# Slot tables of a two-layer hybrid trunk kernel: attention tiles, modulation blocks, first merge level and v products at other slots, solved blocks written back one weight unit earlier in layer 1, decay rows loaded at a later slot

## What is computed

```python
mod_lat = jax.nn.silu(c) @ w_ada + b_ada                 # also for c_ctx
p = (rmsnorm(x, norm_w) * (1.0 + sc) + sh) @ w_in        # combined projection
a = p[:, :, 0] - lam * p[:, :, 1]                        # group A: two softmaxes, then @ v
m = einsum(k_beta, k) * decay; m = tril(m, -1) + eye     # group B: gated delta rule, chunks
sol = triangular_solve(m, rhs)                           # then a scan over the chunks, both ways
x = x + gt * (concat([y_a, y_b]) @ w_out)
```

## Time and profile before

| | |
|---|---|
| median of 3 runs | 2437.49 us (2430.56 to 2441.39) |
| the profiled execution, its own time | 2437.82 us |
| its span, first to last instruction | 2436.0 us |
| PE busy | 2208.2 us, 91% |
| DVE busy | 1416.7 us, 58% |
| ACT busy | 917.3 us, 38% |
| a head of layer 0, 517.80 to 650.62 us | 132.82 us, of which DVE busy 79.89 |
| a head of layer 1, 1621.76 to 1731.32 us | 109.56 us, of which DVE busy 71.10 |
| mean granted clock of TensorE | 0.958 |

### The profile page before, as it was taken

How to read it: one execution, slowest core, us unless ns; L and a number is a source line. 1 busy time by engine, 2 the same in 40 slices (tenths; PEclk the granted TensorE clock), 3 DMA queues, 4 the chain that set the end, 5 groups by cost and what they waited for, 6 DMA issues and landing times. The chain is left out here.

```text
span 2436.0 us, 37434 instructions
## 1 busy us (share of the span) xinstructions
PE 2208.2 (91%) x13100; PEld 1759.9 (72%) x13100; DVE 1416.7 (58%) x2923; ACT 917.3 (38%) x1689; POOL 143.3 (6%) x183
## 2 busy tenths in 40 slices
PE   6789999999999999999999789798988889898887
PEld 3167787877778686868788668686777768686886
DVE  0233656656574757465664555657666575757675
ACT  3432424342433324242522364242424343342533
POOL 0000000000001000000100300000000001000002
PEclk8989999999999999999999889899999989999998
DMA  8974535354443535353645434343424353443664
GB/s 312 350 231 115 169 99 153 89 144 117 114 142 112 153 95 162 98 162 97 193 135 156 155 87 139 106 130 87 142 75 134 84 138 99 110 123 97 170 170 127
DMA packets 503952, 339.24 MB, mean 139 GB/s; under 512 B 63858, under 2 KB 465430, under 8 KB 503366
## 3 DMA queue, kind: packets, MB, share of 16 engines
q1 hardware_dynamic: 408854, 230.13, 33.5%
q10 hardware_dynamic: 94992, 108.09, 13.6%
q0 software_dynamic: 32, 0.07, 0.0%
HBM read 312.99 MB, written 25.23 MB: 139 GB/s over the span
## 5 line engine op out<-in xcount | busy, mean ns | idle before, releaser
L1795 PE MATMUL ps<-h_hi,w_hi 128*128 128x512 f32 (+1 forms) x2080 | 829.6, 399 | 18.1 <-DVE w_lo L1099 10.2
L1797 PE MATMUL ps<-h_hi,w_lo 128*128 128x512 f32 (+1 forms) x2080 | 772.3, 371 | 0.0
L1796 PE MATMUL ps<-h_lo,w_hi 128*128 128x512 f32 (+1 forms) x2080 | 771.8, 371 | 0.0
L1099 DVE TENSOR_TENSOR w_lo<-w_raw,w_hi 128x1024 fp32r<-128x1024 f32 (+1 forms) x300 | 365.5, 1218 | 269.6 <-ACT w_hi L646 226.4
L1795 PEld LDWEIGHTS ps<-h_hi,w_hi 128*128 128x128 f32 x2080 | 403.3, 194 | 131.2 <-issue 55.6
L1797 PEld LDWEIGHTS ps<-h_hi,w_lo 128*128 128x128 f32 x2080 | 400.9, 193 | 70.1
L1796 PEld LDWEIGHTS ps<-h_lo,w_hi 128*128 128x128 f32 x2080 | 404.1, 194 | 50.8
L646 ACT CAST w_hi<-w_raw 128x1024 fp32r<-128x1024 f32 (+1 forms) x300 | 311.4, 1038 | 340.0 <-PE ps L1797 121.3
L2083 PE MATMUL ps<-h_hi,w_hi 128*128 128x512 f32 (+1 forms) x448 | 157.3, 351 | 14.6 <-DVE h_lo L1099 8.5
L2085 PE MATMUL ps<-h_hi,w_lo 128*128 128x512 f32 (+1 forms) x448 | 151.7, 339 | 0.0
L2084 PE MATMUL ps<-h_lo,w_hi 128*128 128x512 f32 (+1 forms) x448 | 151.6, 338 | 0.0
(11 more groups left out here) (196 smaller groups left out, 2562.2 us busy)
## 6 DMA issues: line engine op xcount, KB each, us to landing
w_raw<-in_w_in SPq DMA_DIRECT2D x260, 512.0 KB, 4.1
ada_raw<-in_w_ada ACTq DMA_DIRECT2D x128, 512.0 KB, 4.8
w_raw<-in_w_out SPq DMA_DIRECT2D x36, 448.0 KB, 3.8
arena<-in_w_ada SPq DMA_DIRECT2D x27, 512.0 KB, 8.3
arena<-in_w_out SPq DMA_DIRECT2D x28, 448.0 KB, 3.9
w_raw<-in_w_ada SPq DMA_DIRECT2D x19, 512.0 KB, 8.4
ada_raw<-in_w_ada SPq DMA_DIRECT2D x18, 512.0 KB, 8.4
arena<-decay_rows ACTq DMA_DIRECT2D x16, 512.0 KB, 5.2
```

The source lines that it names most:

```text
L1099: return V.tensor_tensor(o, a, b, op)
L1795: mm(o, w_hi[:, s, k], h_hi[:, kt, t0:], start=kt == 0, stop=False)
L1796: before_last = mm(o, w_hi[:, s, k], h_lo[:, kt, t0:], start=False, stop=False)
L1797: last = mm(o, w_lo[:, s, k], h_hi[:, kt, t0:], start=False, stop=kt == KT - 1)
```

## The change

The offsets TURN_P and ATTEND become tables of slots, and `a_mix` gets a table of its own, MIX. The numbers change as in the diff. In layer 0 the second to fourth query tile stand one slot later, and the first tile's `turn_p` and `attend` as well; `ada(2)` goes from slot 16 to 18, `ada(3)` from 20 to 23; the first level goes from 31 to 32, `v_mul(0)` and `v_mul(1)` one later. In layer 1 the second query tile goes from slots 25, 29, 31, 33 (score, mix, turn, attend) to 27, 32, 34, 36, `a_mix(0)` from 7 to 8, `ada(1)` from 16 to 18, the first level from 33 to 36, the v products two later, O_SLOT one. `blocks_back` of layer 1 stands before unit 11 and no longer before unit 12. `load_g` leaves `q_grow` (slot 8) for slot 26 in both layers. No instruction is added or taken away.

```diff
--- before.py
+++ after.py
@@ -441,17 +441,21 @@
         QUAD = (slice(0, WIDE), slice(WIDE, 2 * WIDE))
         TURN_BACK, GRAM = {0: 4, 1: 5}, {0: 6, 1: 7}
         PIECES = 10
-        SUBST, SOLVED, LEVEL0 = {0: 14, 1: 15}, {0: 29, 1: 31}, {0: 31, 1: 33}
-        CORNERS = {0: 36, 1: 38}
-        V_SLOT = {0: (40, 45, 50, 55), 1: (42, 46, 50, 54)}
-        O_SLOT = {0: 57, 1: 57}
-        SCORE, TURN_P, ATTEND = {0: (3, 12, 21, 30), 1: (4, 25)}, {0: 6, 1: 6}, {0: 8, 1: 8}
+        SUBST, SOLVED, LEVEL0 = {0: 14, 1: 15}, {0: 30, 1: 34}, {0: 32, 1: 36}
+        CORNERS = {0: 37, 1: 41}
+        V_SLOT = {0: (41, 46, 50, 55), 1: (44, 48, 52, 56)}
+        O_SLOT = {0: 57, 1: 58}
+        SCORE = {0: (3, 13, 22, 31), 1: (4, 27)}
+        MIX = {0: (7, 17, 26, 35), 1: (8, 32)}
+        TURN_P = {0: (10, 19, 28, 37), 1: (11, 34)}
+        ATTEND = {0: (12, 21, 30, 39), 1: (13, 36)}
+        LOAD_G = 26
         TABLE_PE, TABLE_ACT = {0: (2, 5, 8), 1: (9, 16, 20)}, {0: (3, 6, 8), 1: (10, 17, 20)}
         TABLE_DVE = {0: (2, 4, 6, 8), 1: (9, 14, 16, 18)}
-        TURN_OA = {0: 42, 1: 38}
-        ROTATE = {0: (45, 47), 1: (41, 43)}
-        ADA_SLOT, ADA_EARLY = {0: (8, 12, 16, 20, 50, 54), 1: (10, 16)}, {0: 4, 1: 2}
-        BLOCKS_OUT, BLOCKS_BACK = {0: 7, 1: 7}, {0: 11, 1: 12}
+        TURN_OA = {0: 43, 1: 40}
+        ROTATE = {0: (46, 48), 1: (44, 46)}
+        ADA_SLOT, ADA_EARLY = {0: (8, 12, 18, 23, 51, 55), 1: (10, 18)}, {0: 4, 1: 2}
+        BLOCKS_OUT, BLOCKS_BACK = {0: 7, 1: 7}, {0: 11, 1: 11}
 
         Y_GROUPS = (slice(0, 4), slice(4, 7), slice(8, 12), slice(12, 15))
         Y_STEPS = len(Y_GROUPS) + 2
@@ -856,8 +860,6 @@
                     def q_grow():
                         nc.scalar.activation(q_dec[:, :, c0:], g_row[:, :, c0:], ACT.Exp).then_inc(q_grown, 1)
                         act.wait_ge(q_grown, h())
-                        if not (isinstance(i, int) and i == HEADS):
-                            load_g(i, 0)
 
                     def k_scale():
                         act.wait_ge(qk_normed, h())
@@ -1005,15 +1007,17 @@
                         put(7 if project else 1, evacuate_z, -1, ZB)
                         put(8, q_grow)
                         put(10, k_scale)
+                        if project:
+                            put(LOAD_G, load_g, i, 0)
                         for j in range(4):
                             put(V_SLOT[layer][j], v_new_copy, j)
                         put(O_SLOT[layer] + 1, o_squares)
                         put(63, y_store, 1)
                         for n, s in enumerate(SCORE[layer]):
                             put(s + 1, exps, n)
-                            put(s + TURN_P[layer], p_copy, n)
-                            put(s + ATTEND[layer], oa_copy, n)
-                        put(SCORE[layer][-1] + ATTEND[layer] + 1, oa_squares)
+                            put(TURN_P[layer][n], p_copy, n)
+                            put(ATTEND[layer][n], oa_copy, n)
+                        put(ATTEND[layer][-1] + 1, oa_squares)
                         put(TURN_OA[layer] + 2, y_store, 0)
                     if project:
                         for t in (AV, BQ, BK, AK, BV):
@@ -1523,7 +1527,7 @@
                         put(10, q_decay)
                         for n, s in enumerate(SCORE[layer]):
                             put(s + 1, a_max, n)
-                            put(s + TURN_P[layer] - (3 if layer and n == 0 else 2), a_mix, n)
+                            put(MIX[layer][n], a_mix, n)
                         for n in range(PIECES):
                             put(SUBST[layer] + n, solve_blocks, n)
                         put(SOLVED[layer], turn_inv, 0)
@@ -1541,7 +1545,7 @@
                         put(O_SLOT[layer] + 2, ob_sums)
                         put(O_SLOT[layer] + 4, ob_norm)
                         put(63, y_out, 1)
-                        put(SCORE[layer][-1] + ATTEND[layer] + 1, oa_sums)
+                        put(ATTEND[layer][-1] + 1, oa_sums)
                         put(TURN_OA[layer] - 1, oa_norm)
                         put(TURN_OA[layer] + 1, y_out, 0)
                     if project:
@@ -2050,8 +2054,8 @@
                         put(O_SLOT[layer] + 5, turn_ob)
                         for n, s in enumerate(SCORE[layer]):
                             put(s, score, n)
-                            put(s + TURN_P[layer], turn_p, n)
-                            put(s + ATTEND[layer], attend, n)
+                            put(TURN_P[layer][n], turn_p, n)
+                            put(ATTEND[layer][n], attend, n)
                         put(TURN_OA[layer], turn_oa)
                     if project:
                         for n, s in enumerate(ROTATE[layer]):
```

## The result

| | before | after |
|---|---|---|
| median of 18 runs each | 2435.37 us (2427.56 to 2442.28) | 2448.07 us (2443.13 to 2452.45) |
| ratio, 95% interval | 1 | 1.0053 [1.0043, 1.0062] |
| the profiled execution, its own time | 2437.82 us | 2449.83 us |
| its span | 2436.0 us | 2447.8 us |

The account below looks back on a forecast made before the run. It took the kernel as a loop over PE, busy 91%, and DVE, whose a_mix PE awaits at turn_p. Terms -8.5 - 3.5 - 3 = -15 from 2437.8, plus 1 for small waits, gave 2424 us, range 2400 to 2452.

Parts of the forecast that it names:

- First heads: First head of each layer: waits for w_ada blocks shrink by 2.7 us each; -5 and -3.5, together -8.5 us.
- Layer 0, forecast -3.5: Seven overlapped heads: scattered waits go, a new one of about 4 us stands at turn_p(2); 0.5 us a head gained.
- (1.23 + 0.19): Layer 0: price in us of the split_lo ahead of a_mix(2), its time and a short gap.
- Layer 1, forecast -3: Seven overlapped heads, loop over PE and DVE: four terms summing to -0.4 us a head, ends -17 and +14 in all.
- Terms 1 to 3: Layer 1, per head: PE's part of the loop shorter, -4.1; DVE's longer, +4.0; elimination sooner, -1.1 us.
- term 4: Layer 1's short slots: three more waits of about 0.5 us, the one at v_mul(1) goes; +0.8 a head, -0.7 to +2.
- The wait for the second `w_ada` block: Layer 1's ada(1), two slots later, was to have no idle time before it; 5.90 us in the first head before.
- The rest: Decay-row load free, sooner blocks_back covered by slack, last bodies 1 us less at turn_p(1) and 1 more at the end: 0.
- the -1.1: Layer 1, per head: elimination starts sooner, its blocks no longer sharing queues with the decay rows; ends 0 and -1.6 us.
- The slower one: Layer 0: w_ada block asked sooner delays the elimination's blocks, making the gathered wait dearer; 2447 or 2454 us, chance 0.20.
- The other half: Slower rival's clock part, layer 0: full 3.3 us of low clock behind the one gathered wait, +6 us in all.
- The faster rival: Layer 0: DVE reaches a_mix(2) in time, so waits and low clock go; 2389 to 2411 us, chance 0.20.

Follow-up runs that it names:

- best3: best2 with layer 0's transpose of the fourth modulation block at slot 30 and its add at slot 31; 0.9973 of the kernel before, 2425.89 us.
- ada_t_later: The change with layer 0's transpose of the fourth modulation block at slot 30 instead of 25, its add at 31 instead of 26; 1.0058 of the kernel before.
- issue_later: ada_t_later with ScalarE issuing layer 0's two DMAs of the fifth w_ada block at slot 26, behind the cast; 1.0040 of the kernel before.
- ob_sooner: The change with VectorE's ob_norm of layer 1 at slot 61 instead of 62, no TensorE slot moved; 1.0017 of the kernel before.
- o57: The change with layer 1's o_mul back at slot 57 and its last v product at 55 instead of 56; 0.9998 of the kernel before.
- best1_v_late: best1 with the change's v products (44, 48, 52, 56) and o_mul (58) in layer 1; 1.0040 of the kernel before, 2442.43 us.
- best1: The change with layer 0's third and fourth modulation multiplies at slots 17 and 21, and layer 1 as before; 0.9943 of the kernel before, 2420.91 us.
- best2: best1 with layer 1's second modulation block at slot 18 instead of 16; 0.9934 of the kernel before, 2418.19 us.
- load_g_early: The change with the load of the decay rows back at slot 8; 1.0103 of the kernel before.
- load_g_only: The kernel before with only the load of the decay rows moved, from slot 8 to slot 26; 0.9994 of the kernel before.

## Why the prediction was wrong

**First heads: right.** Forecast -5 and -3.5; the stretch up to `turn_v` fell by 4.2 us, the way between the layers by 2.4.

**Layer 0, forecast -3.5, measured +8.0.** The shape was right: the scattered waits go, one of about 4 us comes, set by DVE's `a_mix(2)`, and PE would reach `turn_p(2)` 51.0 us behind `turn_v` (50.6 in `best3`, its start at 54.69 less 4.07 of waiting). That it showed at `ada_t`, three slots early, was missed, but `ada_t_later` shows that the place alone moved no time. The low clock behind it, set at 2.5 us a head, was right too: by the clock records it takes 17.2 us of PE's working time in the seven heads, 2.5 each (14.4 before).

**The step that failed** is the price of the `split_lo` that `a_mix(2)` now stands behind, "(1.23 + 0.19)". The 0.19 is the gap that it had behind a tap; in the change it waits for ACT, 1.81 us in six heads, 1.74 on average. I had followed DVE's queue through the move and not ACT's, where slots 23 and 24 now put `exps(2)`, the copy and two DMA issues ahead of that cast. `a_mix(2)` ends 2.75 us later than before, where the forecast's own sum gave 0.7. Of the 2.05 between them 1.55 is this wait, and `issue_later`, which moves nothing but the issues, brings 1.38 of it back. 0.43 is the start of the elimination, 25.97 to 26.40 us behind `turn_v`, of which I had said that it hardly moves. 0.57 is a credit taken too high: the wait of 1.13 us at the `split_lo` of slot 22 did fall to 0.19, but it was that of the one head in the earlier trace rows; the seven average 0.54 before and 0.17 after. Some 0.5 goes the other way, 0.2 of it shorter waits at `a_max(2)`, the rest not taken apart. 7 x 2.05 = 14 us, for 11.5 of error.

**Layer 1, forecast -3, measured +15.3.** Terms 1 to 3 gave -4.1 + 4.0 - 1.1 = -1.2 a head up to `turn_p(1)`. It started 51.75 us behind `turn_v` before and 54.47 after, means of seven heads: 2.72 later against three slots of 4.08, -1.4. The pieces hold too: the cast for `split_lo` kept DVE waiting 1.2 us there (1.1 forecast), the elimination started 2.1 us sooner (the most I had allowed was 1.6), and only the wait at `turn_p(1)` came out otherwise, 6.8 to 8.7 us where 8 to 11 and longer than before was forecast. At `o_mul` the gain still stands (97.29 against 98.09 and one short slot of 0.68: -1.5). Then it is lost: `turn_ob` is at 105.11 against 103.69 + 0.68, +0.7, and the head ends +2.2. So **term 4** was mis-sized: +0.8 a head, -0.7 to +2 at the ends, and it is 1.5 + 2.2 = +3.7. I had seen that "a DVE step and a `split_lo`" come ahead of `turn_ob` and priced that at 0.5 us. It is a wait of 2.28 us, 1.2 of it by these two and the rest by `ob_sums`, which moved as well, plus some 1.5 us behind `turn_ob`, about what 3.4 us at half clock cost (1.7), which I had booked in layer 0 and nowhere in layer 1. `ob_sooner` (6.7 us of layer 1 back), `o57` (12.0) and `best1_v_late` show that this term, and not the attention tiles, carries layer 1's loss. Over its seven heads PE has 3.8 us more idle time and 8.0 us more of low clock in its working time; the 3.5 us left of the 15.3 are in neither.

**The wait for the second `w_ada` block** in layer 1 was to vanish; 13.1 us of waits for these blocks stay, in front of the longer one at `turn_p(1)`. Between `best1` and `best2`, which differ in this block's slot, layer 1 moves by 0.6 us.

**The rest, forecast 0, measured -5.** The last bodies are 5.0 us shorter; in `o57` the gain is 2.3, in `best1`, with before's layer 1, nothing, so it belongs to the layer-1 numbers. The decay rows were given no term of their own outside the -1.1; `load_g_early` prices them at 12 us of gain in the new order, `load_g_only` at nothing in the old one.

**The rivals.** The slower one came in by its outcome, not its mechanism. It had the gathered wait dearer because the `w_ada` block asked sooner would delay the blocks; the elimination of layer 0 starts 0.4 us later and waits for no DMA in the change, so that half is refuted (with the rows at slot 8 the queues do collide, but that is no case of this rival). The other half, the full 3.3 us of low clock behind one gathered wait, did not come either: it is the 2.5 us of the forecast. Layer 0's 8.0 us are 5.1 of idle time and 2.8 of low clock more than before.

The rule of the Trainium skill (TensorE: Matmul & The Clock Gate, "Loop structure matters more than you think") stands beside this rival: long waits between matmuls are what hurts. The runs agree in part. A wait of 2.29 us at `turn_ob` had the clock at 0.50 behind it, and the window behind `turn_ob` before, with no wait, 1.00; but in `best1_v_late` one of 2.38 us had 1.00 behind it. And by `best2` and `best3` the place of a wait can decide more than its length.

The faster rival, that DVE keeps up, is refuted by `ada_t_later`. Two of the forecast's sums are off by themselves: this rival's terms, 29.8 + 14 + 8.5, make 52 us and not 40, and 14 of 19 us of the forecast's 0.38 are 0.28 and not 0.26.
